# A new order of seven block products, with low parts, sines and convolution sums moved, in a one-core Trainium2 decoder layer

## What is computed

```python
h = rmsnorm(x, ln_pre)
c_val, c_glu, c_gate, q, k, v, a_gate, g_conv, g_attn = split_columns(h @ w_in)
u  = c_val * sigmoid(c_glu)
c  = causal_depthwise_conv(u, w_dw, taps=31) + b_dw
ya = (silu(layernorm(c)) @ w_pw * silu(c_gate)) @ w_br_conv
yb = (sliding_window_attention(rope(q), rope(k), v) * silu(a_gate)) @ w_br_attn
m  = sigmoid(g_conv) * ya + sigmoid(g_attn) * yb
x  = x + rmsnorm(m @ w_out, ln_post)
x  = x + sigmoid(x @ w_ple_gate) * (p @ w_ple_proj)
```

## Time and profile before

| | us |
|---|---|
| median of 3 executions (1155.39 to 1156.76) | 1156.72 |
| the profiled execution's own time | 1154.67 |
| its span, first to last instruction | 1152.9 |
| TensorE busy / idle in the span | 1109.1 / 43.8 |
| VectorE busy | 946.6 |
| ScalarE busy | 482.8 |
| GpSimd busy | 316.3 |

### The profile page before, as it was taken

One profiled execution on the slowest core, in us unless ns is written; L12 is line 12 of the kernel. 1 busy time (PEld: TensorE's weight loads), 2 busy tenths in 40 slices (PEclk: granted clock), 3 DMA queues, 4 the chain that ended last, 5 costly groups with the idle time before them and its releaser, 6 DMA issues.

```text
span 1152.9 us, 16104 instructions
## 1 busy us (share of the span) xinstructions
PE 1109.1 (96%) x6040; PEld 898.0 (78%) x6040; DVE 946.6 (82%) x1092; ACT 482.8 (42%) x909; POOL 316.3 (27%) x218
## 2 busy tenths in 40 slices
PE   9799999999999949989999999999999999999998
PEld 8677777777777838867777788888888888888887
DVE  6998989989999996989888589769767968557776
ACT  6524343343433211157666443332536435444332
POOL 2067778787865941520000000000000000000000
PEclk9999999999999979999999999999999999999999
DMA  9802131221314213277871211236454653334555
GB/s 351 318 0 73 37 140 43 76 107 37 110 40 161 74 42 69 52 191 212 214 199 57 73 37 55 78 126 225 149 167 133 231 208 112 125 119 139 178 202 182
DMA packets 49540, 148.21 MB, mean 129 GB/s; under 512 B 5536, under 2 KB 6304, under 8 KB 47424
## 3 DMA queue, kind: packets, MB, share of 16 engines
q1 hardware_dynamic: 35648, 92.77, 23.9%
q10 hardware_dynamic: 11520, 37.75, 9.3%
q0 software_dynamic: 2304, 16.78, 6.0%
HBM read 119.37 MB, written 41.94 MB: 140 GB/s over the span
## 4 chain that ended last, share of the span: by engine, by line
PE 83%; DVE 8%; DMA 3%; ACT 2%; POOL 1%; issue 1%; SPq 1%; DVEq 0%; ACTq 0%; POOLq 0%
PE psg L740 35%; PE psg L927 23%; PE psb L1170 10%; PE psg L1078 6%; DVE last_sums L2037 3%; PE psb L992 1%; PE psg L1049 1%; PE psg L1170 1%; DMA conv<-xT 1%; DMA x_rows<-x_rows 1%; PE psg L793 1%; PE psg L1123 1%; PE psg L1010 1%; ACT kept L1434 1%; PE psg L1044 1%
## 5 line engine op out<-in xcount | busy, mean ns | idle before, releaser
L2037 DVE SCALAR_TENSOR_TENSOR psb<-conv,cols,psb 128x1021 f32<-128x1021 f32 (+6 forms) x196 | 232.9, 1265 | 0.0
L927 PE MATMUL psg<-early_hi,pair_w 128*128 128x512 f32 x448 | 139.4, 392 | 10.9 <-ACT kept L1434 10.9
L1229 POOL TENSOR_TENSOR pair_w<-early_raw,pair_w 128x512 fp32r<-128x512 f32 x91 | 125.2, 1381 | 62.0 <-ACT pair_w L1422 61.7
L740 PE MATMUL psg<-h_hi,w_hi 128*128 128x512 f32 x320 | 101.0, 397 | 23.5 <-POOL w_lo L1222 23.5
L927 PEld LDWEIGHTS psg<-early_hi,pair_w 128*128 128x128 f32 x448 | 83.0, 188 | 33.1 <-POOL pair_w L1229 15.2
L1212 POOL TENSOR_TENSOR rstd<-mean_sq,expo 128x4 f32<-128x4 f32 x3 | 3.1, 1021 | 381.0 <-DVE mean_sq L1874 363.4
L927 PE MATMUL psg<-h_hi,pair_w 128*128 128x512 f32 x336 | 103.5, 389 | 0.0
L1860 DVE TENSOR_TENSOR w_lo<-w_raw,w_hi 128x1024 fp32r<-128x1024 f32 x55 | 67.3, 1224 | 41.1 <-ACT w_hi L1335 40.8
L740 PE MATMUL psg<-h_hi,w_lo 128*128 128x512 f32 x320 | 99.5, 392 | 0.0
L740 PE MATMUL psg<-h_lo,w_hi 128*128 128x512 f32 x320 | 99.4, 392 | 0.0
L740 PEld LDWEIGHTS psg<-h_hi,w_hi 128*128 128x128 f32 x320 | 60.6, 191 | 37.5 <-issue 17.2
(11 more groups left out here) (338 smaller groups left out, 2598.7 us busy)
## 6 DMA issues: line engine op xcount, KB each, us to landing
w_raw<-weights SPq DMA_DIRECT2D x68, 512.0 KB, 3.4
gates<-ring ACTq DMA_DIRECT2D x24, 512.0 KB, 3.6
w_sums<-w_pairs POOLq DMA_DIRECT2D x12, 1024.0 KB, 7.8
ring<-gates ACTq DMA_DIRECT2D x24, 512.0 KB, 4.4
block_raw<-w_sums SPq DMA_DIRECT2D x32, 256.0 KB, 3.0
early_raw<-w_pairs SPq DMA_DIRECT2D x7, 1024.0 KB, 5.3
block_raw<-w_pairs SPq DMA_DIRECT2D x24, 256.0 KB, 3.6
early_raw<-w_pairs SPq DMA_DIRECT2D x7, 768.0 KB, 4.3
```

Of the source, the lines that this page charges most:

```text
L740: mm = nc.tensor.matmul(psg[:, slot, h * HALF:(h + 1) * HALF], w[:, wslot, (wk + k) * P:(wk + k + 1) * P], r[:, k, h * HALF:(h + 1) * HALF ...
L927: mm = nc.tensor.matmul(bank, pair_w[:, at_w, w, k * P:(k + 1) * P], r[:, k, :], start=(not onto and k == 0 and m == 0), stop=(k == KP - 1 ...
L1229: nc.gpsimd.tensor_tensor(pair_w[:, at_w, 1, :], early_source(s, n), pair_w[:, at_w, 0, :].bitcast(F32), ALU.subtract).then_inc(early_spli ...
L2037: own.step(stt(dst, row[:, 0:S - shift], tap(shift), dst, ALU.mult, ALU.add))
```

## The change

- `ORDER` becomes P1, Q5, P6, P2, P7, Q3, P4. GpSimd's order in a set, ScalarE's place for one tanh, VectorE's places for take 0 and the taps follow.
- The low parts of weight tiles 2 and 3 go from GpSimd to VectorE, after its first and fourth block sum; ScalarE makes the high part of tile 2, and the first tanh, ahead of the high parts of the block sums. `plain_input(0)` moves between the block sums and writes to `sums` instead of a row of `conv`; the first convolution row is read from there. GpSimd clears `sums` in set 3 instead of at the start.
- ScalarE takes the sines after query tile j=0; GpSimd makes the low part of tile `Q0 + 2` before it waits for them, and two `add_to_mean` come two tiles later.
- `last_sums` is gone: all eight rows are summed in `psb`, and the first `scores` wait for all eight. Steps: 2 after the first input row, 13 (14 in odd sets, 11 in VAL sets) in a set, 48, and then all that is left. The `taps` calls in attention go (none of the 256 steps was left for them: 11 + 11x13 + 3x11 + 48 + 26 = 261).

```diff
-ORDER = (P1, P2, Q5, P6, P7, Q3, P4)
+ORDER = (P1, Q5, P6, P2, P7, Q3, P4)
...
-        def conv_sums(q, n):
-
-            if q == KT - 1:
-                return last_sums[n][:]
+        def conv_sums(n):
+
             return psb[:, 2 * n:2 * n + 2, :].rearrange("p b s -> p (b s)")
...
-                    pe.wait_ge(conv_done, KT - 1)
+                    pe.wait_ge(conv_done, KT)
...
             low(1)
-            low(2)
-            low(3)
             for s in range(len(EARLY)):
                 early_low(s, P1)
                 early_sum(s, Q5)
-                early_low(s, P2)
                 early_sum(s, P7)
                 early_low(s, Q5)
                 early_sum(s, P6)
+                early_low(s, P6)
+                early_low(s, P2)
                 early_sum(s, P4)
-                early_low(s, P6)
                 early_low(s, P7)
                 early_low(s, Q3)
                 early_low(s, P4)
+                if s == 3:
+                    pool.wait_ge(conv_done, 1)
+                    nc.gpsimd.memset(sums[:], 0.0).then_inc(csum_done, 1)
...
-            add_to_mean(4)
+            low(Q0 + 2)
             pool.wait_ge(sin_ready, 1)
...
-            for t in range(Q0 + 2, C0 - 1):
+            for t in range(Q0 + 3, C0 - 1):
                 low(t)
-            add_to_mean(5)
+                if t in (Q0 + 3, Q0 + 4):
+                    add_to_mean(t - Q0 + 1)
...
+            high(0, 2)
+            product_done(0, 0)
+            nc.scalar.activation(tanh_t[:], psg[:, 0, :], ACT.Tanh, scale=0.5).then_inc(ps_free[0], 1)
             early_sum_high(1, 1)
+            high(0, 3)
             early_sum_high(2, 2)
-            product_done(0, 0)
-            high(0, 2)
-            nc.scalar.activation(tanh_t[:], psg[:, 0, :], ACT.Tanh, scale=0.5).then_inc(ps_free[0], 1)
-            high(0, 3)
...
-                    if n == P6:
+                    if n == P7:
                         early_tanh_of(s, 0)
...
-                if j == 1:
+                if j == 0:
                     act.wait_ge(ang_ready, 1)
...
-            for made, n in enumerate((1, 2, 0, 3)):
-                early_row_sum(n, made)
+            early_row_sum(1, 0)
+            dve.wait_ge(w_lo_ready, PLE_STEPS + 2)
+            tile_low(2)
+            early_row_sum(2, 1)
+            early_row_sum(0, 2)
+            plain_input(0)
+            early_row_sum(3, 3)
+            tile_low(3)
...
-            plain_input(0)
-            taps(11)
+            taps(2)
             plain_input(1)
...
-                    if n == Q5:
-                        dve.wait_ge(early_made, 7 * s + PLACE[Q5] + 1)
+                    if n == P2:
                         early_take(s, 0)
...
-                    if n == Q5:
+                    if n == P2:
                         taps(1 if kind == VAL else 2)
                     elif n == Q3:
-                        taps(0 if kind == VAL else 1)
+                        taps(0 if kind == VAL else 1 + s % 2)
...
-            taps(26)
+            taps(TAPS * KT)
```

More of the change, by code:

```diff
@@ L156, in build @@
         early_rest = at("early_rest", [HALF], F32, GB + 14 * KB)
-        last_sums = [at(f"last_sums{n}", [S], F32, GB + KB * (28 + 4 * n) - 192) for n in range(2)]
         v_last = at("v_last", [P], F32, GB + 24 * KB - 192)
@@ L1206, in _ @@
             own.step(nc.gpsimd.tensor_tensor(rstd[:], ones[:, 0:NB].bitcast(F32), expo[:], ALU.pow))
-            nc.gpsimd.memset(sums[:], 0.0).then_inc(csum_done, 1)
             def rsqrt(n, c=slice(0, NB)):
@@ L1997, in early_row_low, with plain_input @@
                 nc.vector.tensor_tensor(early_lo[:, n], sum_of(n), early_hi[:, n].bitcast(F32), ALU.subtract).then_inc(early_s_ready, 1)
-            for made, n in enumerate((1, 2, 0, 3)):
-                early_row_sum(n, made)
+            def plain_input(q):
+                product_done(q, 1)
+                dve.wait_ge(ps_free[0], KT // 2 + q + 1)
+                if q == 1:
+                    dve.wait_ge(early_s_ready, 4)
+                into = sums[:] if q == 0 else conv[:, CONV_ROWS[q], :]
+                stt(into, tanh_t[:], 1.0, psg[:, 1, :], ALU.add, ALU.mult).then_inc(ps_free[1], 1)
+            early_row_sum(1, 0)
[6 more added lines that the diff above has]
+            tile_low(3)
             dve.wait_ge(tile_done, KT)
@@ L2003, in _ @@
                 early_row_low(n, made + 1)
[L2005 to L2010, removed]
             def conv_steps():
@@ L2018, in tap @@
                         return cols[:, COL_TAPS + i * TAPS + PAD - shift:COL_TAPS + i * TAPS + PAD - shift + 1]
-                    row = conv[:, i, :]
-                    sums_of = (conv_sums(q, 0), conv_sums(q, 1))
+                    out = conv[:, i, :]
+                    row = sums[:] if q == 0 else out
+                    sums_of = (conv_sums(0), conv_sums(1))
                     if q < 2:
@@ L2025, in conv_steps @@
                         dve.wait_ge(u_made, 4 * (q // 2))
-                    if q == KT - 1:
-                        dve.wait_ge(w_lo_ready, PLE_STEPS + V_TILE + 1)
                     if q > 0:
@@ L2039, in conv_steps @@
                     own.wait()
-                    own.step(nc.vector.tensor_scalar(row[:, 0:1], row[:, 0:1], tap(0), col("b_dw", i), ALU.mult, ALU.add))
-                    own.step(stt(row[:, 1:], row[:, 1:], tap(0), sums_of[1][:, 1:], ALU.mult, ALU.add))
+                    own.step(nc.vector.tensor_scalar(out[:, 0:1], row[:, 0:1], tap(0), col("b_dw", i), ALU.mult, ALU.add))
+                    own.step(stt(out[:, 1:], row[:, 1:], tap(0), sums_of[1][:, 1:], ALU.mult, ALU.add))
                     yield
                     own.wait()
-                    nc.vector.tensor_tensor(row[:, 2:], row[:, 2:], sums_of[0][:, 2:], ALU.add).then_inc(conv_done, 1)
+                    nc.vector.tensor_tensor(out[:, 2:], out[:, 2:], sums_of[0][:, 2:], ALU.add).then_inc(conv_done, 1)
                     yield
@@ L2237, in _ @@
                     tile_low(C0 + p // 2 + 1)
-                if p > 1 and p % 2 == 0:
-                    taps(2)
                 if p == 4:
@@ L2248, in _ @@
                 if p == 14:
-                    taps(TAPS)
                     dve.wait_ge(sums_hi_ready, 1)
```

## The result

The changed kernel takes 1110.2 us (median of 4 executions, 1108.77 to 1111.54) against 1156.74 for the kernel before, measured beside it. The ratio is 0.9597, with a 95% interval of 0.9578 to 0.9616: 46.5 us less. The profiled execution was the slowest of its four (1111.54). Against the 1154.67 of the execution profiled before, that is 43.1 us less, where the sum had foretold 42.4.

The account below looks back on a forecast made before the run. TensorE was taken as the bound, its idle 43.8 us and slow matmuls winnable. Terms 9.5 - 0.3 + 14.8 + 18.0 + 0.4 = 42.4 off 1154.67 give 1112.3; plus 2.05 for the median, 1114.3 us; range 1109 to 1124.

Parts of the forecast that it names:

- Sets, 14.8 foretold: In the 14 early sets, the new order removes 1.06 us each, 14.8 us in all, if VectorE keeps up.
- Start, 9.5 less 0.3: At the start, 7.5 us of wait for tile 2's low part and 1.9 of slow clock go; 0.3 lost at Q5.
- The 0.3, or 4.2 at worst: Q5 of the first set delayed by plain_input(1), behind VectorE's low parts of the sums: 0.3 us taken, 4.2 by the shares.
- It costs GpSimd nothing: At the start, VectorE's low parts of tiles 2 and 3 cost GpSimd nothing and VectorE 2.4 us for both.
- Sines, 18.0: In the queries, earlier sines and low part win 16.0 us of wait, 0.1 of overlap and 1.9 of clock.
- Last wait, 0.4: Ahead of the first scores, the 4.0 us wait shrinks to 3.6 us idle: 0.4 won.
- 15.7 us passed: Second rope to first scores took 15.7 us before, 2.1 of them from GpSimd's tile 14 low part holding an addition.
- all of it gone at best: Best case for the wait ahead of the scores: all 4.0 us won.
- VectorE as the bound of the sets: Rival, 12%: VectorE bounds the early sets; at 19.6 us a set, 7.8 us are given back, 1122.
- the steps at the SBUF price: Rival, 3%: PSUM steps cost 1.76 us instead of 1.18; TensorE waits in each set, 80 us lost, 1180 or so.
- a place where nothing happens: Rival, 1%: the change does nothing at one of its places, a wait hidden by another right behind.
- a new wait ahead of the scores: Rival, 8%: low parts or packs late behind moved additions, or VectorE 5 us later than counted: 1119.

Follow-up runs that it names:

- four steps more: The changed kernel with 13 steps in every plain set, so four convolution steps come after the sets, same steps in all: 1122.95 us, ratio 0.9706.
- three low parts by VectorE: The changed kernel with three low parts of the first set (of P7, Q3, P4) made by VectorE instead of GpSimd: 1109.37 us, ratio 0.9591.

## Why the prediction was right, point by point

- **Sets, 14.8 foretold.** Right in mechanism: a pitch of 19.04, 14.0 for the order alone and 13.7 for its undoing, 13.1 in the two profiles. VectorE's lateness in the full sets costs nothing measurable. Most of the missing 1.7 is the wait of 1.5 in the first set, where the prediction had said that none for `kept` would be left.
- **Start, 9.5 less 0.3.** Right in size (9.6 with the input's time taken out, 9.5 alone) and in mechanism: tile 2's low part comes before it is wanted, the clock is 1.00 from 50 to 80 us, where it was 0.89. The 0.3, or 4.2 at worst, was put at the wrong place. Q5 of the first set waited for nothing: the four low parts took 11.10, near the 10.8 of the price that was chosen and far from the 16.3 of the other one, and plain_input(1) came at 75.84 to 77.06, before the 78.4 at which Q5 follows P1. The sentence that failed is "It costs GpSimd nothing". I priced how GpSimd slows VectorE's low parts and not how they slow GpSimd: two sums of 1.3 took 6.52, and over ScalarE's list that became 1.50 of wait at P4. The rule of the Trainium skill that the prediction weighed (SBUF — State Buffer, Who interferes with whom) cuts both ways. Its side for VectorE held; for GpSimd, waiting for one VectorE instruction of 2.3 at each sum of 1.3 gives 3.6, near the 3.26 measured.
- **Sines, 18.0.** Right: of the 21.9 us won between the sets and the scores, 4.0 are the last wait, and 17.9 are left. There is no wait, the low part is made from 380.92 to 383.3 and wanted at 388.6, the clock is 1.00, and the rows are these:

```profile
380.92 2.41 POOL L1218 TENSOR_TENSOR w_lo<-w_raw,w_hi 128x1024 fp32r<-128x1024 f32 x1
383.29 1.90 POOL L1293 TENSOR_TENSOR cos_t<-ring 128x1024 f32<-128x1024 f32 x1
...
390.73 2.41 POOL L1218 TENSOR_TENSOR w_lo<-w_raw,w_hi 128x1024 fp32r<-128x1024 f32 x1 [1.56 <-ACT w_hi L1333]
```

- **Last wait, 0.4.** Here the sum was wrong by 3.6, inside the bound of 4.0 that was named. The count of VectorE's steps held to a microsecond: the last row begins at 397.75, 9.2 behind the end T of query tile 1 (388.6), where 10.0 was foretold; its plain steps take 33.06 (4.83 + 28.23), 1.18 each; the second rope begins at T + 52.2, foretold T + 53.2; TensorE ends the queries at T + 65.2, foretold T + 65.3. What failed is "15.7 us passed ... 2.1 of them because GpSimd's low part held an addition", taken over from the kernel before as if it belonged to the step. Measured: no addition of this rope is held, since the last begins 0.6 us ahead of the low part, and the scores came after at most 8.0 us of unpacking. So no wait was left, and 3.6 more was won: 2.1 for this hold, 1.0 because the rope began that much sooner, and the rest because the unpacking took at most 8.0 us where 8.6 (487.38 to 496.01) had been taken over. The prediction had named this case, "all of it gone at best", but forecast one wait of 2 to 4 us here: for this stretch the forecast missed.
- **The rivals.** VectorE as the bound of the sets, the steps at the SBUF price, and a place where nothing happens: none of them came. (The second was priced too low: cycles of 25.7 and 26.0 us against 19.04 would cost 94 us and not 80, about 1208 and not 1180.) The third, a new wait ahead of the scores with VectorE 5 us late at 1119, is what the kernel with four steps more shows: its profiled run took 1119.18, and its median is 3.8 above that. The margin there is 2.3 us (the rope's rows were issued 7.4 later, the scores began 5.1 later), so a hold by GpSimd or a slower unpacking is enough to open it.
- **The sum.** 43.1 in the profiled pair, 42.4 foretold; by stretches the errors are -1.9 (start, the input's 2.3 among it), -1.7 (sets), +3.5 (queries) and +1.0 (after the scores), so the sum is nearer than its terms, and that nearness is luck. The median forecast of 1114.3 lies 4.1 above the measured 1110.2: 0.8 of it is the sum, 2.1 is what was added for the median of before, and 1.3 is what the profiled execution of after lies above its own.

**Left open.** Why the other executions of the kernel with four steps later lie at 1121 to 1124 where its profiled one took 1119: none of them has a trace. The kernel with three low parts by VectorE is faster than the changed kernel of its own group only; the first measurement of the changed kernel gave 1108.77 to 1111.54, as good. The start was tested whole: what ScalarE's new order brings without VectorE's low parts, or the other way round, was not tried, and neither were the sines without the low part moved ahead of them. And why the input is there up to 2.4 us sooner in some executions (first early matmul from 73.2 to 75.6) was not tried.

## What to carry to other kernels

Two edits whose waits stand one behind the other on TensorE can be worth less alone (9.5 and 4.9) than together (22.1), so test them as one before dropping either. When an operation moves to another engine, price the engine that it leaves beside the one that it goes to: both directions of a shared resource, and what is queued behind it. And a stall copied from the trace of before belongs to the instant at which it happened; shift the instant by a microsecond and it may be gone, or come twice.

## What the runs showed of the hardware

- A run of VectorE instructions with two SBUF inputs seems able to keep GpSimd out until its end, and not for one instruction: 12.38 us for a low part of 2.4, under nine steps of 1.18 (the last row's sums in SBUF). Elsewhere the two engines take turns, one sum of GpSimd's per low part of VectorE's (3.26 us each, in the changed kernel). The Trainium skill's rule (SBUF — State Buffer, Who interferes with whom) speaks of an exclusion for a whole instruction; the 12.38 is more than one, and here the measurement decides. What tells the two cases apart was not tried.
- The unpacking of the second rope, six transfers of 64 KB, took 5.7 and 10.6 us from issue to the scores in two kernels that differ only in when GpSimd made its addition and issued its transfers (8.6 in the kernel before).
